# One normalisation for two, the context prepared earlier, and key and query products tile by tile, between the blocks of a two-block transformer

## What is computed

```python
# end of the first block: x = x + squared_relu_mlp(...)
x = rms_norm(x, norm_final)
# start of the second block
mx = [m[:, None, :] for m in jnp.split(jax.nn.silu(c) @ w_mod + b_mod, 6, axis=-1)]
mc = jnp.split(jax.nn.silu(c_ctx) @ w_mod + b_mod, 6, axis=-1)
hx = modulate(rmsnorm(x, g_norm1), mx[0], mx[1])      # h * (1 + scale) + shift
hc = modulate(rmsnorm(ctx, g_norm1), mc[0], mc[1])
px = jnp.split(hx @ w_in, IN_SPLIT_IDX, axis=-1)      # queries, keys, values, ...
pc = jnp.split(hc @ w_in, IN_SPLIT_IDX, axis=-1)
qx = apply_rope(rmsnorm(heads(px[0])), cos, sin)
kx = apply_rope(rmsnorm(heads(px[1])), cos, sin)
kc = rmsnorm(heads(pc[1]))
```

## Time and profile before

| | |
|---|---|
| median of 3 runs | 3479.39 us (3475.63 to 3484.31) |
| the profiled execution | 3479.53 us, of which the span 3477.7 us |
| TensorE busy | 3217.9 us, 93% |
| VectorE / ScalarE / GpSimd busy | 1540.8 / 997.9 / 496.8 us |
| last matmul of the first feed-forward block to the first matmul of win 4 | 50 us, from 1703.0 to 1753.1 |
| first to last tile of win 4 | 26.9 us, 1753.1 to 1780.0 |

### The profile page before, as it was taken

How to read it: one execution, slowest core, us unless ns; L and a number is a source line. 1 busy time by engine, 2 the same in 40 slices (tenths; PEclk the granted TensorE clock), 3 DMA queues, 4 the chain that set the end, 5 groups by cost and what they waited for, 6 DMA issues and landing times. The chain is left out here.

```text
span 3477.7 us, 37541 instructions
## 1 busy us (share of the span) xinstructions
PE 3217.9 (93%) x15883; PEld 2631.5 (76%) x15883; DVE 1540.8 (44%) x1736; ACT 997.9 (29%) x1290; POOL 496.8 (14%) x342
## 2 busy tenths in 40 slices
PE   7889999998989999999968999989969899999998
PEld 5778787777868888888746665778768788888886
DVE  7444544445356544333354675444653322222224
ACT  6444444434231111111332333222222211111111
POOL 4333231333100000000110000213331000000001
PEclk9999999999999999999987999999989999999999
DMA  3111110011223333111201000100112111111111
GB/s 123 31 43 43 37 37 31 25 43 61 91 70 118 110 121 97 46 46 49 91 31 44 8 8 27 31 31 13 37 55 103 37 49 47 51 43 48 49 46 58
DMA packets 77240, 185.08 MB, mean 53 GB/s; under 512 B 7056, under 2 KB 28944, under 8 KB 77072
## 3 DMA queue, kind: packets, MB, share of 16 engines
q1 hardware_dynamic: 77072, 182.67, 16.5%
HBM read 164.10 MB, written 15.79 MB: 52 GB/s over the span
## 5 line engine op out<-in xcount | busy, mean ns | idle before, releaser
L491 PE MATMUL ps<-b 128*128 128x512 f32 x5928 | 1473.3, 400 | 48.1 <-DVE b L1258 14.9
L491 PEld LDWEIGHTS ps<-b 128*128 128x128 f32 x5928 | 1097.6, 191 | 264.5 <-issue 27.0
L1454 PE MATMUL ps<-b 128*128 128x512 f32 x2592 | 608.5, 395 | 0.5 <-DVE b L1585 0.5
L1454 PEld LDWEIGHTS ps<-b 128*128 128x128 f32 x2592 | 485.0, 187 | 119.1 <-DVE b L1585 1.0
L480 DVE TENSOR_TENSOR b<-b 128x1024 fp32r<-128x1024 f32 (+1 forms) x206 | 274.4, 1333 | 332.7 <-ACT b L472 326.0
L2748 PE MATMUL ps<-b 128*128 128x512 f32 (+1 forms) x1584 | 365.0, 387 | 37.2 <-DVE b L1808 14.4
L472 ACT ACTIVATE b<-b 128x1024 fp32r<-128x1024 f32 (+1 forms) x206 | 215.2, 1046 | 566.3 <-PE ps L1454 464.1
L2748 PEld LDWEIGHTS ps<-b 128*128 128x128 f32 x1584 | 284.7, 198 | 95.3 <-issue 42.7
L1323 POOL TENSOR_TENSOR b<-b 128x1024 f32<-128x1024 f32 x24 | 57.6, 2400 | 1647.0 <-ACT b L1329 1646.6
L1170 POOL TENSOR_TENSOR b<-b 128x512 f32<-128x512 f32 x112 | 151.0, 1361 | 516.2 <-DVE b L1074 394.7
L1500 ACT ACTIVATE b<-ps 128x1024 f32<-128x1024 f32 x54 | 55.5, 1028 | 389.1 <-PE ps L491 389.1
(11 more groups left out here) (285 smaller groups left out, 3377.0 us busy)
## 6 DMA issues: line engine op xcount, KB each, us to landing
b<-in_down SPq DMA_DIRECT2D x52, 512.0 KB, 3.7
b<-in_mod SPq DMA_DIRECT2D x96, 256.0 KB, 2.7
b<-in_gu SPq DMA_DIRECT2D x44, 512.0 KB, 3.6
b<-scratch SPq DMA_DIRECT2D x38, 512.0 KB, 4.4
b<-in_dn_in SPq DMA_DIRECT2D x32, 512.0 KB, 5.1
b<-in_up SPq DMA_DIRECT2D x32, 512.0 KB, 3.8
b<-in_win SPq DMA_DIRECT2D x26, 512.0 KB, 3.7
scratch<-b SPq DMA_DIRECT2D x18, 512.0 KB, 3.0
```

Of the source, the lines that this page charges most:

```text
L491: ins = e.matmul(ps[:, c], w, h[:, k, c], start=first and k == 0 and i == 0, stop=last and k == KT - 1 and i == 2)
L1454: ins = e.matmul(ps[:, c], w, u[:, at[k], c], start=k == 0 and p == 0, stop=k == n - 1 and p == 2)
```

## The change

It has four parts. **(1) One factor.** Beside the sum of squares of x, a second one, of norm_final times x, is taken in the last down group; from both, the combined factor of two norms follows, and `wfa` = norm_final times the modulation's gain is the column factor. ScalarE squares every tile twice (`act_stat2`), GpSimd accumulates twice (`pool_stat2`), TensorE sums with two columns of ones instead of 128 (`pe_stat2`). The stored, once normalised x is now made after the tiles for the product, behind the conversion of win 1. **(2) The context beside the feed-forward block.** Its loads, squares, sums and normalisation follow the modulation in the `beside` generator, at steps 50 to 62. **(3) Keys and the first queries together.** `pe_between` runs win 4 and win 0 tile by tile, then the context's keys; ScalarE copies the three results out, then converts win 1. **(4)** Chains 0 and 1 start with both products done. Buffers move: `z` gets three buffers in the between part, and the ones of the attention lie on the right side.

```diff
 def attention_projections(side):
-    yield from side.project(("win", 4))
-    side.ready.add(0)
-    for m in range(4):
+    side.ready |= {0, 1}
+    for m in range(1, 4):
...
+    def pe_stat2(self, e, m, sig):
+        ones = self.con("ones")[:, 0:2]
+        for last in range(2):
+            for c in range(2):
+                e.wait_ge(*(A.at("sq", "d", KT - 1, c) if last else G.at("acc", "d", KT - 2, c)))
+                b = m["sq"][c] if last else m["accs"][c]
+                for n in range(8):
+                    at = 16 * c + 2 * n
+                    ins = e.matmul(self.psl[3][:, at:at + 2], blk(b, n), ones, start=at == 0 and not last, stop=last == 1,
...
+    def act_stat2(self, e, m, sig, k):
+        for c, w in ((0, 1.0), (1, self.par("norm_final")[:, k:k + 1])):
+            if k >= 2:
+                e.wait_ge(*G.at("acc", "d", k - 1, c))
+            e.activation(m["sq"][c] if k else m["accs"][c], m["x"][:, k, :], ACT.Square, scale=w).then_inc(*A.up("sq", "d", k, c))
...
# pe_modulation
+        for k in range(KT):
+            if k % 2 == 0:
+                yield
+            e.wait_ge(*V.at("mt", 11))
+            e.wait_ge(*A.at("sq", "c", k))
+            for b in range(2):
+                ins = e.matmul(S[:, 2 * b:2 * b + 2], blk(self.c_sq[k % 2], b), self.con("ones")[:, 0:2],
...
+        yield
+        e.wait_ge(*V.at("rc", "c"))
+        rows(e, S[:, 512:768], self.st[:, 32:34], self.con("ident")).then_inc(*P.up("rw", "c"))
...
# act_modulation
+        for k in range(KT):
+            if k % 2 == 0:
+                yield
+            e.wait_ge(*self.xl[k].at("ctx"))
+            if k >= 2:
+                e.wait_ge(*P.at("cs", "c", k - 2))
+            e.activation(self.c_sq[k % 2], self.c_x[:, k, :], ACT.Square).then_inc(*A.up("sq", "c", k))
...
     def pe_between(self, e):
+        e.wait_ge(*V.at("rc"))
+        rows(e, self.psl[2], self.st[:, 8:16], ident).then_inc(*P.up("rw"))
+        rows(e, self.psl[3], self.st[:, 0:8], ident).then_inc(*P.up("rw", "f"))
+        for k in range(KT):
+            e.wait_ge(*(G if k % 2 else V).at("l", k))
+            for i, j in enumerate((j4, j0)):
...
+                for part in range(2):
+                    ins = self.gemm_piece(e, self.psl[i], j, k, part, self.b_hi, self.b_lo)
...
# act_between, behind the eight tiles
+        e.wait_ge(*P.at("keys"))
+        e.activation(self.z[0][:, TC:TA], self.psl[0], ACT.Copy).then_inc(*Q.up("ev", k4, 0))
+        e.wait_ge(*self.gm.at(UNIT[q0]))
+        e.activation(self.z[1], self.psl[1], ACT.Copy).then_inc(*Q.up("ev", q0, 0))
+        e.wait_ge(*self.gm.at(UNIT[k4]))
+        e.activation(self.z[0][:, 0:TC], self.psl[2][:, 0:TC], ACT.Copy).then_inc(*Q.up("ev", k4, 2))
+        self.act_weights(e, UNIT[k4] + 3)
...
# dve_between, behind the eight tiles
         self.dve_weights(e, UNIT["win", 4] + 3)
-        self.after_between(e)
+        e.wait_ge(*V.at("z", KT - 1))
+        e.wait_ge(*P.at("rw", "f"))
+        for k in range(KT):
+            x = self.x1[:, k, :]
+            e.scalar_tensor_tensor(out=x, in0=x, scalar=self.par("norm_final")[:, k:k + 1], in1=self.psl[3],
+                                   op0=ALU.mult, op1=ALU.mult).then_inc(*V.up("y", k))
...
     def sp_qkv(self, e):
+        e.wait_ge(*self.aq[1].at("ev", ("win", 4), 2))
```

More of the change, by code:

```diff
@@ L398, in memory @@
+        with second:
             with ExitStack() as at:
[L399 to L402, removed]
+                self.qs = [sb([128, 4, T], F32R, at, "right") for _ in range(2)]
+                self.ks = [sb([128, TA], F32R, at, "right") for _ in range(2)]
+                self.kx = [sb([128, TA], F32R, at, "right") for _ in range(2)]
+                self.vx = sb([128, 10, 192], ctx=at, side="right")
@@ new lines, in dve_modulation @@
+        e.tensor_tensor(self.wfa, self.ax, self.par("norm_final"), ALU.mult).then_inc(*V.up("wfa"))
+        for k in range(0, KT, 2):
+            yield
+        yield
+        st = self.st
+        e.wait_ge(*P.at("cs", "c", KT - 1))
+        e.tensor_scalar(st[:, 32:34], S[:, 0:4:2], 1.0 / D, EPS, ALU.mult, ALU.add).then_inc(*V.up("ms", "c"))
+        e.wait_ge(*A.at("rt", "c"))
+        e.reciprocal(st[:, 32:34], st[:, 34:36]).then_inc(*V.up("rc", "c"))
+        for k in range(KT):
+            yield
+            z = self.c_x[:, k, :]
+            e.wait_ge(*P.at("rw", "c"))
+            e.scalar_tensor_tensor(out=z, in0=z, scalar=self.ac[:, k:k + 1], in1=S[:, 512:768], op0=ALU.mult,
+                                   op1=ALU.mult).then_inc(*V.up("z", "c", k))
@@ new lines, in dve_between @@
+    def dve_between(self, e):
+        P, A, V, G = self.b2
+        st, sums = self.st, self.psl[3]
+        e.tensor_scalar(st[:, 0:8], sums[:, 0:16:2], 1.0 / D, EPS, ALU.mult, ALU.add).then_inc(*V.up())
+        e.wait_ge(*V.last())
+        e.tensor_scalar(st[:, 36:44], st[:, 0:8], EPS, None, ALU.mult).then_inc(*V.up())
+        e.wait_ge(*V.last())
+        e.scalar_tensor_tensor(out=st[:, 8:16], in0=sums[:, 16:32:2], scalar=1.0 / D, in1=st[:, 36:44], op0=ALU.mult,
+                               op1=ALU.add).then_inc(*V.up("ms"))
+        e.wait_ge(*A.at("rt"))
+        e.reciprocal(st[:, 0:16], st[:, 16:32]).then_inc(*V.up("rc"))
+        e.wait_ge(*P.at("rw"))
+        for k in range(KT):
+            z = self.n_z[k % 3]
+            if k >= 3:
+                e.wait_ge(*(G if (k - 3) % 2 else V).at("l", k - 3))
+            e.scalar_tensor_tensor(out=z, in0=self.x1[:, k, :], scalar=self.wfa[:, k:k + 1], in1=self.psl[2],
+                                   op0=ALU.mult, op1=ALU.mult).then_inc(*V.up("z", k))
@@ L2740, in piece @@
         ctx = with_context(u)
-        if u == ("win", 4) and part == 0:
-            e.wait_ge(*s.b2[2].at("l", "c", k))
-            e.wait_ge(*s.b2[3 if k % 2 else 2].at("l", "x", k))
         for p, i, last in piece_steps(k, part, ctx):
```

218 lines of the change are left out of this document (99 added, 119 removed).

## The result

| | before | changed |
|---|---|---|
| median of 4 runs | 3480.22 us | 3504.15 us (3499.59 to 3506.39) |
| ratio | | 1.0067 (95% interval 1.0050 to 1.0085) |
| the profiled execution | 3479.53 us, span 3477.7 | 3506.39 us, span 3504.6 |

The changed kernel is slower by 24 us (0.7%). I read the result as some 27 us, between 24 and 30. The forecast was 16.9 us more, 3496.

A forecast was written before the change was run, and what follows sets the result against it. TensorE, busy 93% of the span, bounds the kernel in the first feed-forward block, a chain of norms between the blocks. Sum A +31.4 and sum B -14.5 give +16.9 us on 3479.53: 3496 us, range 3485 to 3506.

The forecast's parts named there:

- The pauses: First feed-forward block: TensorE waits four times 3.8 us for ScalarE's context squares, once 2.0 us for the reciprocal.
- The clock behind them: Half clock after TensorE's waits in the first feed-forward block: 2.2 us lost for each of four, 0.7 for the fifth.
- sum A: The context beside the first feed-forward block makes it 31.4 us longer, bounds 22 and 37.
- The rival with the clock kept: First feed-forward block: waits leave TensorE's clock full, sum A is 22.6 us, the kernel 3487.6 us; 14%.
- The sums for x: TensorE's sums of squares at the block's end: 32 calls at 0.23 us, 7.3 us in all.
- sum B: From the block's last matmul to the second query row's head sums: 14.5 us gained, bounds 9 and 19.
- The tile loop: Between the blocks: eight tiles keep their earlier pace, 30.8 us, some 7 us a pair.
- The wait for win 3: Before the first head sums: TensorE idle 14.8 us, as win 3 loads behind x's stores and rope tables.
- From there to chain 2: From TensorE going on after win 3 at 1771.2 to the second query row's head sums at 1811.9.
- win 3 in time: Rival, between the blocks: the loads cost ScalarE nothing, sum B is about 29 us, the kernel 3482 us; 5%.
- hidden pauses: Rival, first feed-forward block: squares made early, sum A is 4.0 + 2.3 us, kernel faster by 8 us; 7%.
- B gives nothing: Rival, tile loop: low clock makes TensorE set the pace, up to 15 us lost, 3511 us; 5%.

The follow-up runs named there:

- second chip: The changed kernel, without an edit, measured again against the kernel before on another chip: slower by 29.7 us, ratio 1.0086.
- E1: Changed kernel with TensorE summing the context squares one step later than ScalarE makes them: 3476.9 us, 1.0004 times the kernel before.
- E3: Changed kernel with SP's load of win 3 ahead of the stores of x: 3493.7 us, 1.0059 times the kernel before.
- E4: Changed kernel with VectorE's eight scalings of x for storing ahead of its low part of win 1: 3487.8 us, 1.0042 times the kernel before.
- F3: Changed kernel with win 3 loaded before the stores, x scaled right behind the last tile, win 1 converted at the between part's start: 3486.2 us, ratio 1.0024.
- F2: Changed kernel with the context's squares, sums and tiles four steps later on every engine: 3477.6 us, 1.0003 times the kernel before.
- G2: G1 with TensorE's sums at the block's end in 48 records instead of 64: 3449.8 us, 0.9927 times the kernel before.
- G1: F4 with the conversion of win 1 ahead of the wait for all engines: 3451.3 us, 0.9930 times the kernel before.
- G3: G2 with VectorE making all low parts in the tile loop, GpSimd none, and each high part one ScalarE instruction: 3442.7 us, ratio 0.9907.
- F4: F3 with TensorE's context sums one step later as in E1: 3455.6 us, 0.9940 times the kernel before.

## Why the prediction was right, and where its sizes were off

Slower was right, and so were the mechanism and its places. The size was 7 us short (16.9 against 24 by the first pair of medians), and both sums erred to the same side; against the second chip's 29.7 it was 13 short. At chain 2, the point that I had summed to, the change was +29.4 us, above the +28 which both upper bounds together gave. That the median, 3504, still lies within 3485 to 3506 is in part luck: 2.5 us come back behind chain 2, and the first pair of medians lies closer together than the traces and the second pair.

**The pauses** were right in number, place and cause: 3.8 us forecast, 3.86 found, four times, and 2.0 against 1.82 for the reciprocal. The short matmuls and the spread were forecast at 4.0 us and cost 4.0 (E1).

**The clock behind them** is the mis-sized term of sum A: 9.5 us forecast, 14.0 measured. I had read 5.8 and 4.4 us at half clock behind two waits and counted from where the matmuls begin. But in both the clock had already fallen in the wait; stretches inside the first and the second in the kernel before (columns as above) are

```profile
1007.30:1009.70 2.40, 0.00 (x0) 0.00 (x0) 2.30 (x5) 1.97 (x2) 0.00 (x0) 1.00 0.42 164
1009.85:1010.70 0.85, 0.00 (x0) 0.00 (x0) 0.85 (x2) 0.00 (x0) 0.00 (x0) 0.50 0.00 0
...
2335.00:2336.00 1.00, 0.00 (x0) 0.00 (x0) 0.96 (x2) 0.00 (x0) 0.00 (x0) 0.50 0.00 0
```

The full one is 6.8 us in both places, as behind the new pauses, and what falls into the wait costs nothing. How much that is differs from place to place and is the same each time: in the five traces with these pauses (changed twice, E3, E4, F3) the unit behind the second takes 12.78 to 12.83 us and the one behind the third 13.97 to 14.06. What sets it stays open. The cost is up to 3.4 us a pause, and I took 2.2 for each, with 3.4 as the bound. The 2.0 us wait got 0.7 and cost 1.7 (3.4 us at half clock, all on matmuls), although F2, without pauses ahead of it, shows the same wait at no cost. The rival with the clock kept (14%) is out.

**The sums for x** are the largest miss of sum B: 7.3 us forecast, 11.9 measured. I had the 0.23 us a call from head sums at full clock. Here the clock fell 2 us into the line:

```profile
1740.40:1750.00 9.60, 9.60 (x46) 9.52 (x45) 0.00 (x0) 1.29 (x2) 0.00 (x0) 0.50 0.01 2
```

46 records in 9.6 us are 0.21 us each, against 0.11 before it fell. I had doubled the calls and not asked whether the clock would hold through them, with 1.97 us for the spread "at a reduced clock" in my own rows. G2 shows the term by itself: 16 records less are 3.4 us less (7.94 us, 11.36 in G1). How early the clock falls in this line varies: in ten traces the same 64 records take 9.95 us (F2, where it falls after 4.2 us) to 11.89 (F3). With it the first scaling came 15.0 us behind the block, forecast 9.9.

**The tile loop** was right: 30.8 us from the first scaling to the last tile, forecast 30.9. That GpSimd sets its pace was in the rows, and I did not see that it does so by holding up VectorE too (G3).

**The wait for win 3** was right in cause and nearly in size: 16.3 us, forecast 14.8. From the last tile to the end of the wait it took 29.2 us, forecast 27.4: the stores and tables were issued 1.2 us later than I had them, and the rest is the load's landing. E3 and E4 confirm the cause from two sides.

**From there to chain 2** it took 42.6 us, forecast 40.7. Chain 0's rotation matmuls (L1967) are among it, at half clock: 3.53 us, where chain 1's take 1.90; the rest was not followed. Together 5.1 - 0.1 + 1.8 + 1.9 = 8.7 us less gain in B than the 14.6 I had summed: 5.9, below my lower bound of 9.

The rivals with win 3 in time and with hidden pauses did not occur, but they were the right edits: F3 is the one, E1 the other. For both together the prediction says 3459; by its own terms (6.3 - 29) it is 3457, and F4 measured 3455.6. "B gives nothing" did not occur either: the tile loop kept its pace. The gain was still small (5.9 us), and 4.6 us of what was missing are the sums ahead of the loop, at half clock.

## What to carry to other kernels

Work put beside a dense stretch of TensorE costs what TensorE waits for it, so let TensorE use its results one step later than the engine makes them; here that one line was worth 28 us. Price a pause there as itself plus up to half of the low-clock stretch behind it (here 3.86 us and up to 3.4), and price a long run of short matmuls at the end of a dense stretch at half clock for most of its length. When a chain is shortened, write down for the new end which load, which PSUM buffer and which conversion must be there in time, and move their issue with it.

## What the runs showed of the hardware that I had not expected

- A pause of 3.86 us brings 6.8 us at half clock even with 48 matmuls queued behind it, and how much of this falls into the pause changes from one pause to the next (none, or 1.5 to 1.6 us), in the same way in five traces.
- The records of two-column matmuls run 0.11 us apart at full clock and 0.21 at half clock. Between dense units eight of them leave the clock alone (E1); 64 in a row run into half clock after 2 us in the changed kernel and after 4 us in F2 (L1338).
- VectorE's instruction with two SBUF inputs takes 2.54 us beside GpSimd's and 1.28 without it; it is part of why a pair of tiles takes 7.0 us in F4 and 5.9 in G3.
